# A hybrid encoder trunk on one core: seven products for four couples of the FFN's down projection in the second 1024 columns too

## What is computed

```python
x = x + rms_norm(mixed, g_mix_post)
f = jnp.square(jax.nn.relu(rms_norm(x, g_ffn_pre) @ w_up)) @ w_down
return x + rms_norm(f, g_ffn_post)
```

## Time and profile before

| | before |
|---|---|
| median of three runs | 1904.34 us (1903.96 to 1905.06) |
| span of the profiled execution | 1903.1 us |
| TensorE busy | 1891.0 us, 99% |
| VectorE busy | 1445.1 us, 76% |
| ScalarE busy | 983.1 us, 52% |
| read from HBM | 377.55 MB |

### The profile page before, as it was taken

How to read it: one execution, slowest core, us unless ns; L and a number is a source line. 1 busy time by engine, 2 the same in 40 slices (tenths; PEclk the granted TensorE clock), 3 DMA queues, 4 the chain that set the end, 5 groups by cost and what they waited for, 6 DMA issues and landing times.

```text
span 1903.1 us, 28366 instructions
## 1 busy us (share of the span) xinstructions
PE 1891.0 (99%) x10022; PEld 1685.3 (89%) x10022; DVE 1445.1 (76%) x1777; ACT 983.1 (52%) x1285; POOL 117.6 (6%) x166
## 2 busy tenths in 40 slices
PE   9999999999999999999999999999999999999998
PEld 7988888988988998898888888889889889989987
DVE  6886768886796688579878757678767966876887
ACT  6455656554445445445554556555544544454443
POOL 3920020000000000000000000200000000000000
PEclk9999999999999999999999999999999999999999
DMA  8665356567558557666576554565766575576563
GB/s 290 203 223 173 118 190 218 181 200 241 183 175 262 178 175 227 215 199 187 210 242 220 180 166 138 183 213 169 234 216 200 187 241 187 172 241 209 184 225 149
DMA packets 168325, 380.79 MB, mean 200 GB/s; under 512 B 11968, under 2 KB 14128, under 8 KB 167728
## 3 DMA queue, kind: packets, MB, share of 16 engines
q1 hardware_dynamic: 167904, 377.58, 61.6%
q10 hardware_dynamic: 336, 2.11, 0.3%
HBM read 377.55 MB, written 2.10 MB: 199 GB/s over the span
## 4 chain that ended last, share of the span: by engine, by line
PE 94%; DVE 3%; DMA 1%; issue 1%; ACT 1%; POOL 0%; DVEq 0%; POOLq 0%; ACTq 0%; SPq 0%
PE acc_pair L548 25%; PE acc_pair L553 13%; PE acc_pair L514 8%; PE acc_pair L848 8%; PE acc_pair L516 8%; PE acc_pair L847 8%; PE acc_pair L515 8%; PE acc_pair L849 8%; DVE w_lo L1356 1%; PE o_bank L766 1%; PE t_bank L849 1%; PE t_bank L848 1%; PE t_bank L847 1%; DVE h_both L1410 1%; DMA raw<-in_w_down 0%
## 5 line engine op out<-in xcount | busy, mean ns | idle before, releaser
L1356 DVE TENSOR_TENSOR w_lo<-raw,w_hi 128x1024 fp32r<-128x1024 f32 x687 | 832.3, 1233 | 251.9 <-ACT w_hi L956 243.2
L956 ACT CAST w_hi<-raw 128x1024 fp32r<-128x1024 f32 x687 | 705.5, 1049 | 503.3 <-DVE raw L1904 119.3
L548 PE MATMUL acc_pair<-h_both,w_hi 128*128 128x512 f32 x2176 | 560.2, 380 | 0.1
L548 PEld LDWEIGHTS acc_pair<-h_both,w_hi 128*128 128x128 f32 x2176 | 371.1, 190 | 30.3 <-ACT proj L1025 0.5
L553 PEld LDWEIGHTS acc_pair<-h_both,w_lo 128*128 128x128 f32 x2176 | 327.4, 190 | 29.1
L553 PE MATMUL acc_pair<-h_both,w_lo 128*128 128x256 f32 x2176 | 330.4, 274 | 0.0
L847 PE MATMUL acc_pair<-w_hi,f_hi 128*128 128x512 f32 x672 | 254.7, 379 | 0.0
L848 PE MATMUL acc_pair<-w_lo,f_hi 128*128 128x512 f32 x672 | 254.7, 379 | 0.0
L849 PE MATMUL acc_pair<-w_hi,f_lo 128*128 128x512 f32 x672 | 254.7, 379 | 0.0
L514 PE MATMUL acc_pair<-w_hi,h_both 128*128 128x512 f32 x444 | 170.5, 384 | 1.7 <-DVE w_lo L1356 1.5
L515 PE MATMUL acc_pair<-w_lo,h_both 128*128 128x512 f32 x444 | 168.3, 379 | 0.0
(11 more groups left out here) (245 smaller groups left out, 1905.4 us busy)
## 6 DMA issues: line engine op xcount, KB each, us to landing
raw<-in_w_up SPq DMA_DIRECT2D x256, 512.0 KB, 4.5
raw<-in_w_down SPq DMA_DIRECT2D x240, 512.0 KB, 4.9
raw<-in_w_in SPq DMA_DIRECT2D x128, 512.0 KB, 4.7
raw<-in_w_out SPq DMA_DIRECT2D x64, 512.0 KB, 5.4
raw_side<-in_w_down SPq DMA_DIRECT2D x16, 512.0 KB, 7.6
x<-in_x SPq DMA_DIRECT2D x8, 256.0 KB, 7.7
w_pool_s<-in_w_pool SPq DMA_DIRECT2D x2, 1024.0 KB, 7.4
post_row<-in_g_mix_post SPq DMA_DIRECT2D x2, 1024.0 KB, 7.4
```

Of the source, the lines that this page charges most:

```text
L548: pe.matmul(acc_pair[b][:, m, :], w_hi[:, slot, col:col + P], x_both.rearrange("p s (a n) -> p s n a", a=2), start=(slot, k) == (0, 0), st ...
L956: act.copy(w_hi[:, half * PAIRS + p, :], raw[:, p, :]).then_inc(hi_made, 1)
L1356: dve.tensor_tensor(w_lo[:, slot, :], src[:, p, :], w_hi[:, slot, :].bitcast(F32), ALU.subtract).then_inc(lo_made, 1)
```

## The change

The second 1024 columns of groups 0 to 2 get seven products at slots 0, 4, 8 and 12 too, with the same slot order and the same sums of activations. For this:

- `t_sum`, `t_hi` and `t_lo` exist twice. The second `t_hi` lies where `act_f` is, the second `t_sum` where `bias` and `over_count` were. These two tables are written to HBM in the first group of layer 0 and read back at its end. ScalarE's rounding of couple 1's sums waits until `act_f` has been read.
- The shared products no longer stay in PSUM. After each stage `shared_sums` copies (group 0) or adds the four banks to `kept_sums`, which takes the place of x. x is written to HBM in group 0 of each layer and read back in the last group, one token half at a time, both on ScalarE's queue.
- In `seven` the first couple's products on the shared banks come ahead of those on `acc_pair`.
- On VectorE `weight_sums(g, 0, 1, ...)` and two weight rests come ahead of `turned_square(g, u, 1)` in the last up unit. At the end of the first columns the sums of the next stage's couples 0 and 1, their rests and `shared_sums` come ahead of `wide_sums`.
- `combine(1, ...)`, for the second columns, runs in the last group's first two up units; `combine(0, ...)` stands where `combine` stood.

```diff
-    x = own("x", [P, T, D])
+    r_x = region(4 * T * D)
+    x = at("x", [P, T, D], F32, r_x)
+    kept_sums = at("kept_sums", [P, T, SHARED, CH], F32, r_x)
...
+    r_t = ((r_qkv + 12 * CH, r_qkv + 24 * CH), (r_qkv, r_tables))
...
                     if first:
-                        pe.wait_ge(acc_free[0], result + 1)
+                        shared_products()
+                        bank_free(0, 0, j, result)
                     three(acc_pair[0][:, 0, :], f_hi[:, k1, early], f_lo[:, k1, early],
                           w_hi[:, s1, left], w_lo[:, s1, left], first, False)
+                    if first:
+                        bank_free(0, 1, j, result)
                     three(acc_pair[0][:, 1, :], sh[:, 3, :], sl[:, 3, :], w_hi[:, s1, right],
                           w_lo[:, s1, right], first, False).then_inc(w_used, 1)
...
                     if first:
-                        pe.wait_ge(acc_free[1], result + 1)
+                        bank_free(1, 0, j, result)
+                    else:
+                        shared_products()
                     three(acc_pair[1][:, 0, :], f_hi[:, k1, late], f_lo[:, k1, late],
-                          t_hi[:, 2, :], t_lo[:, 2, :], first, False).then_inc(t_used, 1)
+                          th[:, 2, :], tl[:, 2, :], first, False).then_inc(t_used, 1)
...
+                def sums_hi(g, j, n):
+
+                    no = seven_no(l, g, j, n)
+                    if (j, n) == (0, 1):
+                        act.wait_ge(flo_made, l * 32 + g * 8 + 8)
                     act.wait_ge(t_step, 3 * no + 3)
...
+                def shared_sums(g, j, first):
...
+                    dve.wait_ge(t_used, 3 * seven_no(l, g, j, len(SEVEN_AT)) - 1)
+                    for k, bank in enumerate((ssa_bank, t_bank[0], t_bank[1], o_bank)):
+                        dst = kept_sums[:, 1 - j, k, :]
+                        if first:
+                            dve.tensor_copy(dst, bank[:, :]).then_inc(shared_free, 1)
+                        else:
+                            dve.tensor_tensor(dst, bank[:, :], dst, ALU.add
+                                              ).then_inc(shared_free, 1)
...
                 def wide_pair(g, j, first, last=False):
 
                     hu = hu0 + HU_F + g * HU_GROUP + 2 * CHUNKS + PAIR_HALVES * j
-                    if j == 0:
-                        seven_lo(g, 2, hu + 2, 0)
-                        seven_lo(g, 3, hu + 3, 1)
-                        split_lo(hu + PAIR_HALVES, 0, (0, 1))
+                    seven_lo(g, j, 2, hu + 2, 0)
+                    seven_lo(g, j, 3, hu + 3, 1)
+                    nxt = hu + PAIR_HALVES
+                    if j == 0 and not last:
+                        weight_sums(g, 1, 0, nxt)
+                        split_lo(nxt, 0, (0, 1))
+                        sums_lo(g, 1, 0)
+                        shared_sums(g, j, first)
+                        split_lo(nxt, 0, (2, 3))
+                        weight_sums(g, 1, 1, nxt + 1)
                         wide_sums(g, j, first)
-                        split_lo(hu + PAIR_HALVES, 0, (2, 3))
-                        split_lo(hu + PAIR_HALVES + 1, 1, src=raw_side if last else raw)
+                        split_lo(nxt + 1, 1, (0, 1))
+                        sums_lo(g, 1, 1)
+                        split_lo(nxt + 1, 1, (2, 3))
+                    elif j == 0:
+                        split_lo(nxt, 0, (0, 1))
+                        shared_sums(g, j, first)
+                        split_lo(nxt, 0, (2,))
+                        wide_sums(g, j, first)
+                        split_lo(nxt, 0, (3,))
+                        split_lo(nxt + 1, 1, src=raw_side)
                     else:
-                        for n in range(PAIR_HALVES - 1):
-                            split_lo(hu + n + 2, n % 2)
-                        split_lo(hu + PAIR_HALVES + 1, 1, (0, 1))
+                        split_lo(nxt, 0, (0, 1))
+                        shared_sums(g, j, first)
+                        split_lo(nxt, 0, (2, 3))
                         wide_sums(g, j, first)
-                        split_lo(hu + PAIR_HALVES + 1, 1, (2, 3))
+                        split_lo(nxt + 1, 1)
...
+                        if u == CHUNKS - 1:
+                            weight_sums(g, 0, 1, hu + u * 2 + 3)
+                            split_lo(hu + u * 2 + 3, 1, (0, 1))
                         turned_square(g, u, 1)
...
                         if u == CHUNKS - 1:
                             s_rest(g, 3)
-                            seven_lo(g, 1, hu + u * 2 + 3, 1)
+                            sums_lo(g, 0, 1)
+                            split_lo(hu + u * 2 + 3, 1, (2, 3))
```

More of the change, by code:

```diff
@@ L849, in three, with bank_free, seven @@
                     return pe.matmul(bank, xl, in_turn(wh), start=False, stop=stop)
-                def seven(g, n, hu, result):
+                def bank_free(t, c, j, result):
+                    pe.wait_ge(acc_free[t], result + (c if j else 1))
+                def seven(g, j, n, hu, result):
                     i = SEVEN_AT[n]
[L854 to L858, removed]
+                    no, s0, s1 = seven_no(l, g, j, n), i % RING, i % RING + 1
+                    k0, k1 = K_ORDER[i], K_ORDER[i + 1]
+                    first, end = n == 0, n == len(SEVEN_AT) - 1
                     left, right = c_cols(0), c_cols(1)
@@ L861, in seven @@
                     sh, sl = s_hi[n], s_lo[n]
-                    pe.wait_ge(flo_made, l * 32 + g * 8 + k1 // 2 + 1)
-                    pe.wait_ge(s_lo_made, no + 1)
+                    th, tl = t_hi[n % 2], t_lo[n % 2]
+                    if j == 0:
+                        pe.wait_ge(flo_made, l * 32 + g * 8 + k1 // 2 + 1)
+                        pe.wait_ge(s_lo_made, (l * FF_GROUPS + g) * len(SEVEN_AT) + n + 1)
+                    if first and not (isinstance(g, int) and l + g + j == 0):
+                        pe.wait_ge(shared_free, shared_done(l, g, j))
@@ L1380, in add_posts @@
                     dve.wait_ge(rstd_ready, l * RS_LAYER + h * (RS_POST1 + T) + t + 1)
+                    if not h and c == 0:
+                        dve.wait_ge(x_back[t], 16 * l)
                     part = acc[:, t, c_cols(c)]
@@ L1906, in seven_lo @@
                     if again:
[L1907 to L1908 removed]
+                        dve.wait_ge(t_used, 3 * no - 4)
+                    dve.tensor_tensor(out[:, 1, :], low_r, out[:, 0, :], ALU.subtract
                                       ).then_inc(t_step, 1)
@@ L1915, in seven_lo @@
+                def seven_lo(g, j, n, hu, half):
+                    weight_sums(g, j, n, hu)
                     split_lo(hu, half, (0, 1))
-                    dve.wait_ge(t_hi_made, no + 1)
-                    dve.tensor_tensor(t_lo[:, :, :], t_sum[:, :, :], t_hi[:, :, :].bitcast(F32),
-                                      ALU.subtract).then_inc(t_lo_made, 1)
+                    sums_lo(g, j, n)
                     split_lo(hu, half, (2, 3))
-                def combine(which):
-                    q1, q5, q6, q7 = (q_sum[:, k, :] for k in range(4))
+                def shared_sums(g, j, first):
+                    if first and j == 0:
+                        dve.wait_ge(x_saved, 16 * T * (l + 1))
+                    dve.wait_ge(t_used, 3 * seven_no(l, g, j, len(SEVEN_AT)) - 1)
[6 more added lines that the diff above has]
+                                              ).then_inc(shared_free, 1)
@@ L1925, in into, with combine @@
+                def combine(j, which):
+                    q7, q1, q5, q6 = (kept_sums[:, 1 - j, k, :] for k in range(SHARED))
+                    base = 16 * l + 8 * (1 - j)
                     def into(t, c, part):
-                        dst = acc[:, t, c_cols(c)]
-                        dve.scalar_tensor_tensor(dst, part, rstd[:, COL_X2 + t:COL_X2 + t + 1], dst,
+                        dst = halves(acc[:, t, c_cols(2 * j + c)])
+                        dve.scalar_tensor_tensor(dst, put_back(part),
+                                                 rstd[:, COL_X2 + t:COL_X2 + t + 1], dst,
@@ L2013, in group @@
                             turned_unit(u)
+                            if last and u < 2:
+                                combine(1, 2 * u)
+                                combine(1, 2 * u + 1)
                     if first:
```

168 lines of the change are left out of this document (103 added, 65 removed).

## The result

| | after | before, run alongside |
|---|---|---|
| median | 1943.28 us (1938.50 to 1948.23, 4 runs) | 1904.41 us (1903.96 to 1905.06, 4 runs) |
| ratio | 1.0204, 95% interval 1.0186 to 1.0221 | |
| span of the profiled execution | 1941.3 us | 1903.1 us |
| mean granted TensorE clock | 0.991 | 0.999 |

The page's first part of the changed kernel (busy us, share of the span, instructions) answers the earlier trace rows. Its waits of TensorE (for whom, us in total, times, longest) answer.

What follows compares the result with a forecast made beforehand. TensorE was taken to bound the kernel, with VectorE's queue order adding waits. Middle groups 16.0, group 0 7.6 and last groups 7.8 us sum to 31.4 over 1904.34: 1936 us, range 1908 to 1950.

Steps and rivals of the forecast that it cites:

- Added: VectorE's new work: per couple four sums and one rest, plus four shared sums (2.4 us) after each of 14 stages.
- (1): Start of first columns, all eight groups: TensorE waits 2.5 us for VectorE's reduction that frees acc_pair[1].
- (2): First columns of a middle group: VectorE ends couple 3's rests 32.2 us after TensorE's first matmul.
- (3): Start of second columns, six times: wide sums start at 46.8 us, first done at 47.5; TensorE waits about 3 to 3.6.
- (4): Start of the next up product: TensorE waits some 0.5 us until both halves of acc_pair[0] are read.
- Transfers: x and tables moved to HBM and back on ScalarE's queue: taken as nothing, at most 3 us a layer.
- Last group: Last group of each layer, no matmul saved: 3.4 us at the second columns plus 0.5 for combining, 3.9 each.
- Wait 1: TensorE's wait in the first columns for the reduction that frees acc_pair[1], forecast at 2.5 us in all eight groups.
- rival C: Waits as forecast, and the clock falls to half rate in the six long ones, 12 us more: 1948 us; chance 0.11.
- wait 2: TensorE's wait for the wide sums at the second columns, forecast at about 3 to 3.6 us, six times.
- A: Rival: no waits come and the dropped matmuls count in full, 15.5 us saved, 1888.8 us; chance 0.10.
- B: Rival: only the 2.5 us wait for the reduction in the first columns comes: +4 us, 1909 us; chance 0.11.

Runs made afterwards that it cites:

- the run with two couples: Changed kernel, but only couples 2 and 3 of the second columns take seven products, the others eight, with VectorE's order as before the change: 1900.73 us, ratio 0.9981.
- second half first: Changed kernel with couple 1's sums and rests put back behind the second half's reduction in the last up unit: 1938.47 us, ratio 1.0176.
- run with fillers: Changed kernel plus overwritten matmuls, nine where TensorE waits in the first columns and fifteen where it waits in the second: 1938.00 us, ratio 1.0176.
- wide sums first: Changed kernel with the wide sums directly behind the shared sums at the end of the first columns, ahead of two rests and four sums: 1937.32 us, ratio 1.0172.

## Why the prediction was right, and which step of it failed

Forecast 1936 (1908 to 1950), slower by over 0.2% with 0.84. Measured 1943.28. By its steps:

- **Removed.** 72 matmuls at 0.2158: confirmed by the count of matmuls and by the run with two couples (1.30 us a stage for six).
- **Added.** VectorE's 24 x 4.3 + 14 x 2.4 = 137 us: its busy time rose by 135.2. The copy out of PSUM, which I put between 0.41 and 0.75, took 0.68, as an addition does, and 0.60 from start to start: the value taken was right.
- **(1)** The reduction at +5.2: measured +4.9, TensorE's next product at +6.2 (forecast 6.4). The wait was 2.0 to 2.5 us in six groups instead of 2.5.
- **(2), (3)** The wide sums at +46.8: measured 594.65 - 547.87 = +46.8, TensorE at +47.6 (forecast 47.5). The late block was there as well (0.66 us). In this group the walk along VectorE's queue was right to 0.1 us. In the other three middle groups the wide sums started at +45.7 to +46.9, in group 0 at +45.2 and +46.0, so over all groups it was right to about 1 us, and the 0.1 is in part luck.
- **(4)** 0.5 us: measured 0.44 to 0.52, in all six.
- **Transfers** at nothing: shown by the run with them alone, for the kernel before.
- **Last group.** +3.9 forecast, +4.9 and +5.0 measured, but for another reason, so that the nearness is luck. Wait 1 was 3.1 us there instead of 2.5, since VectorE began couple 1's sums 1.07 us after TensorE's start and not at 0 (887.08 against 886.01), and the clock took 1.6 more. The late block and the shared sums, my 3.4, cost nothing of their own: TensorE was by then later than VectorE, whose wide sums waited 0.27 us for it. They stand behind wait 1 all the same: with wait 1 taken away (second half first), the last groups' first columns still took 41.4 and 41.8 us instead of 38.85.
- **The clock: the step that failed.** I put it at nothing in the forecast, because the earlier trace rows showed it held for some 4 us behind the last matmul, and left it to rival C. The prediction named a clock below 1.00 within the span as what would make it wrong, and that came: nine falls, 14.3 us. It moved the time by less, since in three groups the same delay shortened wait 2 (4.8 us). That is one part of why the gaps came to 37.5 us (34.1 listed) and not to the 46 forecast; the other parts are wide sums that were ready 0.5 to 1.5 us sooner than in (3) in four groups, and the last groups' extra terms, which did not come on top of wait 1. The run with fillers, in which the clock stays up, gave 1938.0, or 1934.7 without the 3.3 us by which the fillers overran (an estimate from its trace), against the forecast's 1936. So the waits were priced rightly in sum, and the clock's part of 1943.28 is some 9 us, which the forecast lacked. C had the mechanism, at 12 us for six long waits, but added them to waits left as long as before. The measured time is nearer to C's 1948 than to the 1936 of the forecast.

A is out, with 34.1 us of waits, and so is B, since wait 2 came in all six stages.

The Trainium skill (TensorE: Matmul & The Clock Gate, Part 1) would have the clock fall to its lower level on idling; the trace agrees in that, and shows it in the changed kernel at idle gaps from 1.86 us on, though not at all of them. Its spacing of about 216 ns for 512 columns is what the groups show (0.2158), the sustained 131 ns (Back-to-back issue gap) is seen in no stage.

## What to carry over

If work is added on an engine that is only 76% busy, walk its queue against the deadlines of the bound engine: the average left 15 us in a group (146.5 of 161.6), the order left none, and mending the order moved the wait until the work itself was cut. Take the part of the change whose work fits between two deadlines: with three of four couples, and the sums that free PSUM ahead of the rests that wait for other engines, it is 0.33% faster, where all four are 2.0% slower. Reckon with 1.6 us of half clock behind an idle gap of TensorE of some 2 us or more (here it came behind nine of fourteen), but add it in full only where no further long wait follows.

## What I had not expected of the hardware

The clock fell behind nine of the fourteen waits above 1 us in the changed kernel. These nine were 1.86 to 3.09 us long; the five that it survived were 1.24, 1.59, 1.99, 2.13 and 2.29. So length alone doesn't decide: 1.86 cost it and 2.29 did not.

```profile
1685.02 0.48 PE L861 MATMUL acc_pair<-t_hi,f_hi 128*128 128x512 f32 x1 [2.29 <-DVE act_f L1883]
...
1685.99 0.38 PE L862 MATMUL acc_pair<-w_lo,f_hi 128*128 128x512 f32 x1
1686.20 0.38 PE L863 MATMUL acc_pair<-w_hi,f_lo 128*128 128x512 f32 x1
```

Nor does it fall at the wait: behind the wait that ended at 724.35 (2.17 us) five matmuls ran at full speed, and the slow ones began at 725.53. Whether a gap of some 2 us costs the clock, these traces don't settle: with the wide sums first, all eight of wait 1 (1.99 to 3.07 us) did. And matmuls whose result is thrown away made the kernel faster: 162 of them took 5.3 us off the median, where 72 useful ones dropped had been meant to give 15.5.
